# Token rows of a top-2-of-8 expert stage: one transfer over all DMA engines, or transfers of eight rows

## The reference

```
def _moe_swiglu(h, w_router, w_gate, w_up, w_down):
    logits = (h @ w_router).astype(jnp.float32)
    top_v, top_i = lax.top_k(logits, TOP_K)
    top_w = jax.nn.softmax(top_v, axis=-1)
    gates = jnp.sum(jax.nn.one_hot(top_i, N_EXP, dtype=jnp.float32) * top_w[..., None], axis=-2).astype(h.dtype)
    out = jnp.zeros_like(h)
    for e in range(N_EXP):
        out = out + gates[..., e:e + 1] * _swiglu(h, w_gate[e], w_up[e], w_down[e])
    return out
```

## Time and profile before

| what | us |
|---|---|
| three runs | 1407.06, 1409.41, 1410.49 |
| their median | 1409.41 |
| the profiled execution | 1405.8 |
| its span in the profile | 1404.1 |
| PE busy (share of the span) | 1334.4 (95%) |
| PE weight loads busy | 710.5 (51%) |
| VectorE busy | 367.0 (26%) |
| ScalarE busy | 283.4 (20%) |
| GpSimd busy | 103.3 (7%) |

### The profile page before, as it was taken

How to read it: one execution, slowest core, us unless ns; L and a number is a source line. 1 busy time by engine, 2 the same in 40 slices (tenths; PEclk the granted TensorE clock), 3 DMA queues, 4 the chain that set the end, 5 groups by cost and what they waited for, 6 DMA issues and landing times.

```text
span 1404.1 us, 27790 instructions
## 1 busy us (share of the span) xinstructions
PE 1334.4 (95%) x12536; PEld 710.5 (51%) x12536; DVE 367.0 (26%) x459; ACT 283.4 (20%) x363; POOL 103.3 (7%) x181
## 2 busy tenths in 40 slices
PE   4999989999999999999999999999899999998885
PEld 2997777668888885333334433333233333332331
DVE  2666343657445454101000101000101101101104
ACT  3564534453443333000000000000000000000001
POOL 5100131324000001000000000000000000010010
PEclk9999999999999999999999999999999999999999
DMA  9854948899855568999999999999999999999994
GB/s 383 277 169 153 372 189 305 342 401 409 327 197 183 179 233 336 365 414 423 424 424 430 399 423 429 401 423 429 399 424 429 401 425 427 407 424 426 425 428 195
DMA packets 103254, 500.15 MB, mean 356 GB/s; under 512 B 10417, under 2 KB 14206, under 8 KB 74470
## 3 DMA queue, kind: packets, MB, share of 16 engines
q1 hardware_dynamic: 87232, 471.75, 83.6%
q10 hardware_dynamic: 13510, 18.29, 3.6%
q0 software_dynamic: 2400, 8.42, 1.5%
HBM read 478.74 MB, written 19.69 MB: 355 GB/s over the span
## 4 chain that ended last, share of the span: by engine, by line
PE 79%; DMA 16%; DVE 2%; SPq 1%; ACT 1%; issue 1%; DVEq 0%; ACTq 0%
PE ps L2400 30%; PE ps L2429 12%; PE ps L439 6%; PE ps L441 6%; PE ps L440 6%; DMA ring_a<-in_moe_up 4%; DMA ring_a<-in_moe_down 4%; PE ps L2424 3%; DMA ring_b<-in_moe_down 3%; PE ps L1848 2%; PE ps L1834 2%; DMA raw<-in_moe_down 2%; DMA ring_b<-in_moe_up 2%; PE ps L1957 1%; PE ps L1959 1%; PE ps L1958 1%
## 5 line engine op out<-in xcount | busy, mean ns | idle before, releaser
L2400 PE MATMUL ps<-ring_a,hTf 128*32 128x512 f32 (+1 forms) x2160 | 208.6, 541 | 8.9 <-DMA ring_a<-in_moe_up 5.3
L2400 PE MATMUL ps<-raw,hTf 128*32 128x512 f32 (+1 forms) x2064 | 197.5, 538 | 1.8 <-DMA raw<-in_moe_up 1.8
L1782 DVE TENSOR_TENSOR hm<-gate_bc,ps 128x384 f32<-128x384 f32 (+1 forms) x30 | 17.9, 596 | 648.3 <-PE ps L2400 647.6
L380 DVE TENSOR_TENSOR w_lo<-raw,w_hi 128x2048 fp32r<-128x2048 f32 x60 | 149.5, 2495 | 118.0 <-ACT w_hi L376 117.9
L2400 PEld LDWEIGHTS ps<-ring_a,hTf 128*32 128x32 f32 x2160 | 70.4, 110 | 143.7 <-issue 126.9
L2400 PE MATMUL ps<-ring_b,hTf 128*32 128x384 f32 (+1 forms) x1408 | 138.4, 539 | 4.6 <-DMA ring_b<-in_moe_up 2.0
L376 ACT ACTIVATE w_hi<-raw 128x2048 fp32r<-128x2048 f32 x60 | 114.5, 1913 | 122.4 <-PE ps L441 101.7
L2400 PEld LDWEIGHTS ps<-raw,hTf 128*32 128x32 f32 x2064 | 70.6, 110 | 123.5 <-issue 118.8
L439 PE MATMUL ps<-w_hi,hTh 128*128 128x512 f32 x248 | 97.8, 394 | 1.5 <-DVE w_lo L380 1.5
L441 PE MATMUL ps<-w_lo,hTh 128*128 128x512 f32 x248 | 96.6, 389 | 0.0
L440 PE MATMUL ps<-w_hi,hTl 128*128 128x512 f32 x248 | 96.5, 389 | 0.0
(11 more groups left out here) (412 smaller groups left out, 1545.1 us busy)
## 6 DMA issues: line engine op xcount, KB each, us to landing
raw<-in_w_mod SPq DMA_DIRECT2D x48, 1024.0 KB, 9.3
raw<-in_moe_down SPq DMA_DIRECT2D x22, 2048.0 KB, 29.0
ring_a<-in_moe_down SPq DMA_DIRECT2D x20, 2048.0 KB, 22.3
ring_a<-in_moe_up SPq DMA_DIRECT2D x14, 2048.0 KB, 27.1
ring_b<-in_moe_down SPq DMA_DIRECT2D x14, 2048.0 KB, 27.5
raw<-in_moe_gate SPq DMA_DIRECT2D x13, 2048.0 KB, 25.4
ring_a<-in_moe_gate SPq DMA_DIRECT2D x11, 2048.0 KB, 32.6
raw<-in_moe_up SPq DMA_DIRECT2D x10, 2048.0 KB, 20.3
```

Source lines behind the costliest of these rows:

```text
L380: nc.vector.tensor_tensor(w_lo[:, w % SPLIT], raw[:, slot % RAW], w_hi[:, w % SPLIT].bitcast(F32), ALU.subtract).then_inc(s["lo_ready"], 1)
L1782: VT(hm[:, g, 0:w], sgm[at % SILUS][:, 0:w], ps[:, part % 4, 0:w], ALU.mult).then_inc(s["h_ready"], 1)
L2400: last = MM(ps[TOK * j:TOK * j + TOK, part % 4, 0:w], hTf1[:, kt, q * P + TOK * g:q * P + TOK * g + TOK], wt[:, kt % 2, j, :], start=kt == ...
```

## The change

`row_load` issues one transfer for each eight rows in place of one for all rows. With 64, 128, 64, 96, 96, 96 and 64 rows these are 8, 16, 8, 12, 12, 12 and 8 transfers, 76 in place of 7. Each adds 16 to `xrow_loaded`, so PE's wait in `turn_rows` counts 16 for each piece. The bytes are the same, and so is everything else.

```
+ROWS = 8
+LOADS = (0, *(TOK * g // ROWS for g in POS_G[1:]))
+LOAD_SUM = tuple(sum(LOADS[:i + 1]) for i in range(N_EXP))
...
-                src = rows_io.rearrange("(e r) n -> e r n", r=REGION)[e, p * n:p * n + n]
-                sp.dma_start(xrow[0:n, :], src).then_inc(s["xrow_loaded"], 16)
+                rows_e = rows_io.rearrange("(e r) n -> e r n", r=REGION)
+                for r in range(0, n, ROWS):
+                    sp.dma_start(xrow[r:r + ROWS, :], rows_e[e, p * n + r:p * n + r + ROWS]).then_inc(s["xrow_loaded"], 16)
...
-                pe.wait_ge(s["xrow_loaded"], 16 * ((N_EXP - 1) * p + i))
+                pe.wait_ge(s["xrow_loaded"], 16 * (LOAD_SUM[N_EXP - 1] * p + LOAD_SUM[i]))
```

## The result

The changed kernel takes 1413.14 us (median of 15 runs, 1408.31 to 1416.86), the kernel before 1406.75 us (15 runs, 1404.52 to 1410.49). The ratio is **1.0046, 95% interval 1.0035 to 1.0056**: slower by 6.4 us where 7 us less were forecast. It lies within the stated range only by the rival of the late half. The profiled execution took 1412.1 us, its span is 1410.4, 6.3 more than before.

The account below looks back on a forecast made before the run. The prediction took the slowest DMA engine's last weights to bound the kernel. Terms −5 −2 = −7 took the profiled 1405.8 to 1398.8 us; with the median 3.6 above, 1402.4 us, range 1396 to 1417.

Parts of the forecast that it names:

- the rival of the late half: End of the weights: the eight engines taking rows are the late ones; +3.9 us, 1413.3 us, chance 0.18.
- What bounds the kernel: End of the expert stage: set by when the slowest DMA engine has delivered its last weights.
- Term 1: End of the weights: row loads shift to eight engines, taken as the early ones, relieving the late ones; −5 us.
- the eight are the late ones: Rival, end of the weights: late half gets +5.9, stall −2; +3.9, 1413.3 us, chance 0.18.
- Term 2: Row loads beside the weight stream: stall falls to 0.015 us a row, 9 us from 11; −2 us.
- Terms 3 and 4: SP's 69 more issues are covered by queued work; PE's turning of rows has slack; 0 each.
- term 4: PE's turning of rows: 6.3 us smallest slack, rows land sooner if the engines are early; 0.
- The two slower rivals: Row loads: stall doubles for each row (+12, 1421.4 us, chance 0.13); queue at two destinations (about +30, 1439 us, chance 0.06).

## Why the prediction was wrong

**What bounds the kernel** was read rightly: the engine that ends last sets the end. Every experiment moved with the last landing, with 15.7 to 15.9 us behind it in each.

**Term 1 is the step that failed.** It weighed "the eight that get the rows are those that end at 1377" against "the eight are the late ones", as if early and late had to be the two halves by number. Rows 5 gave only how many engines are late, eight, not which; I took equal counts for equal sets. The eight that take rows are six early and two late. The arithmetic of the shift was sound; only the 0.5 us for more completions has no row behind it, and 38 transfers cost nothing that could be measured (1.0006). The six early ones end near 1383 (1382.9 was worked out), the six late ones that are relieved with them (1382.5), and the two that are late and take rows too end at 1388.4 + 5.9 = 1394.3; measured 1394.7. One engine on the wrong side is enough: what counts is the latest, so the relief of the others was worth nothing. The two early engines that take no rows gained nothing either: they should have ended near 1371 and reported at 1377.5 and 1378.6. The last weight transfer was issued 6.3 us later (1354.97 against 1348.69), since SP waits until the unit that was in the buffer before has been used; that this held the two is argued, not shown.

**Term 2** (-2) came out between 0 and +1.7: the slices lose 11.4 us in six loads where five lost 9.7 and the 128-row load nothing, and the last landing leaves 0.4 us for it (6.3 less 5.9). That a load's stall is one price per row with fewer partitions dearer was the wrong variable. What goes with the cost, in the runs with 128 rows, with strides and with rows four apart, is an engine writing partitions that are not its own in the weight transfers. The 128-row load was free before because it has the weight transfers' own pattern, and lost that when it was cut.

**Terms 3 and 4** held at 0: SP's issues take 7.7 us at the worst place and stay covered, PE never waits for xrow. A free issue took 0.28 us and not 0.34. The last row load didn't land sooner, as term 4 had it for early engines, but 7.2 us later (1236.4 against 1229.2); PE had 4.4 us to spare.

**The sum** with these two put right is +5.9 + 0; the span grew by 6.3.

**The rivals.** "The eight are the late ones" had the right mechanism for the two engines that matter, and gave 1413.3 us; measured 1413.14. That agreement is luck: it stands on a median of before of 1409.41, where 15 runs gave 1406.75, and on a stall term of -2 that did not come. The loss was 6.4 us where it gave 3.9. Its picture would have left six more engines late. The two slower rivals, on narrow destinations, fell: four rows side by side were no worse than eight, and eight apart no better. The rule to use all 16 engines of the Trainium skill ("DMA: Bandwidth & Descriptors", section "Rules for kernel authors"), weighed in the prediction, would have put the sum between 0 and 5.9; the measured sign is on its side, though what decided here, two late engines among the eight, is not in it.

## What to carry to other kernels

When a transfer is moved to some of the DMA engines, ask of each of them how late it is, not of the group: the latest engine decides, and a step in the DMA share at the end tells only how many are late. The updates of the semaphores do tell: those of a weight transfer give the spread of all sixteen, those of a load with few engines say how many of its own are late, and a cheap run with 4, 6 and 8 rows sorts them. A load beside a weight stream at full rate should have the stream's pattern over the partitions: 128 rows with a third of them useless were cheaper than 64 or 96 rows.

## What the runs showed that I had not expected

- Loads of 64 or 96 rows cost 1.5 to 2.2 us each of the full rate beside the weight transfers, 128 rows don't, and eight-row transfers don't either when each engine writes the partitions that it writes anyway.
- TensorE's program weighs on eight of the sixteen engines: 67 fetches of 16 KB in 830 us; without 24 of them, and their matmuls, the lag of the eight is 2.9 us shorter, and the kernel by about as much.
- GpSimd's instructions are fetched over one engine. 6144 semaphore increments on an otherwise idle GpSimd cost a kernel bound by DMA 16 us.
